# Picked tokens fetched by number, and a changed order in the heads, the convolution and the end of the merge, in a two-layer diffusion step

## What is computed

```python
g = jax.nn.sigmoid(gt.reshape(bsz, n_tok, N_BRANCH, D_MODEL))
merged = g[:, :, 0] * (y_ml @ w_pa) + g[:, :, 1] * (y_cv @ w_pb) + g[:, :, 2] * (y_na @ w_pc)
return merged @ w_o, (c_s, n_s, m_s), nk, nv

def expert_choice_ffn(h, w_router, w_gate, w_up, w_down):
    cap = EC_CAPACITY_FACTOR * n_tok // N_EXPERTS
    aff = jax.nn.softmax((h @ w_router).astype(jnp.float32), axis=-1)
    gate, idx = lax.top_k(jnp.swapaxes(aff, 1, 2), cap)
    xg = jax.vmap(lambda hb, ib: hb[ib])(h, idx)
    a = jnp.einsum('becd,edf->becf', xg, w_gate)
    u = jnp.einsum('becd,edf->becf', xg, w_up)
    y = jnp.einsum('becf,efd->becd', jax.nn.silu(a) * u, w_down) * gate[..., None].astype(h.dtype)
    return jax.vmap(lambda yb, ib: jnp.zeros((n_tok, d), h.dtype).at[ib.reshape(-1)].add(
        yb.reshape(-1, d)))(y, idx)
```

## Time and profile before

| | us |
|---|---|
| median of 3 runs | 3190.81 |
| lowest, highest | 3184.38, 3193.99 |
| the profiled execution | 3193.39 |
| its span, first to last instruction | 3191.6 |
| mean granted clock of PE | 0.951 |
| PE busy, DVE busy, ACT busy, POOL busy in the span | 2995.6, 1876.5, 1357.6, 546.3 |

### The profile page before, as it was taken

How to read it: one execution, slowest core, us unless ns; L and a number is a source line. 1 busy time by engine, 2 the same in 40 slices (tenths; PEclk the granted TensorE clock), 3 DMA queues, 4 the chain that set the end, 5 groups by cost and what they waited for, 6 DMA issues and landing times.

```text
span 3191.6 us, 42921 instructions
## 1 busy us (share of the span) xinstructions
PE 2995.6 (94%) x17920; PEld 2461.0 (77%) x17920; DVE 1876.5 (59%) x2079; ACT 1357.6 (43%) x1751; POOL 546.3 (17%) x218
## 2 busy tenths in 40 slices
PE   4999989999997999999989998899999799999998
PEld 2979877999896676767659798899999766676765
DVE  4542644324316989888865427341351488989897
ACT  2133230111106767777741432310110577777775
POOL 2413213233211000000024133152332100000000
PEclk7989899999988999999989898799998799999999
DMA  8523447557514989898985234332443198989896
GB/s 232 73 34 60 87 113 198 131 161 172 136 70 147 345 285 343 279 346 282 344 225 75 32 64 83 73 67 40 80 80 113 55 348 296 327 296 329 300 324 235
DMA packets 357650, 580.80 MB, mean 182 GB/s; under 512 B 13712, under 2 KB 148880, under 8 KB 357328
## 3 DMA queue, kind: packets, MB, share of 16 engines
q1 hardware_dynamic: 297488, 501.26, 53.8%
q10 hardware_dynamic: 51808, 56.53, 5.6%
q0 software_dynamic: 8160, 20.26, 2.0%
HBM read 568.54 MB, written 9.45 MB: 181 GB/s over the span
## 4 chain that ended last, share of the span: by engine, by line
PE 76%; DVE 8%; DMA 7%; issue 3%; ACT 2%; DVEq 2%; SPq 1%; ACTq 0%; POOL 0%; POOLq 0%
PE ps L826 27%; PE ps L1310 8%; PE ps L1313 8%; PE ps L1318 8%; PE ps L792 5%; DMA ring<-w_down 3%; PE ps L1227 2%; DVE w_lo L2242 2%; PE ps L868 2%; PE ps L1088 2%; DVEq L1969 2%; DMA ring<-w_gate 1%; PE ps L900 1%; ACT w_hi L1440 1%; PE ps L1005 1%
## 5 line engine op out<-in xcount | busy, mean ns | idle before, releaser
L2242 DVE TENSOR_TENSOR w_lo<-ring,w_hi 128x2048 fp32r<-128x2048 f32 x256 | 584.3, 2287 | 99.3 <-ACT w_hi L1440 98.6
L826 PE MATMUL ps<-h_hi,w_hi 128*128 128x320 f32 x1792 | 560.2, 313 | 3.7 <-DVE arena L2020 2.0
L826 PE MATMUL ps<-h_lo,w_hi 128*128 128x320 f32 x1792 | 555.6, 310 | 0.0
L826 PE MATMUL ps<-h_hi,w_lo 128*128 128x320 f32 x1792 | 555.6, 310 | 0.0
L1440 ACT ACTIVATE w_hi<-ring 128x2048 fp32r<-128x2048 f32 x256 | 486.6, 1909 | 82.7 <-DMA ring<-w_up 24.5
L671 POOL CAST w_hi<-ring 128x2048 fp32r<-128x2048 f32 (+1 forms) x76 | 143.0, 1881 | 1607.0 <-DMA ring<-w_in 1007.6
L1500 ACT ACTIVATE arena<-ps,par 128x640 f32<-128x640 f32 x88 | 70.0, 796 | 705.3 <-PE ps L826 675.7
L673 POOL TENSOR_TENSOR w_lo<-ring,w_hi 128x2048 fp32r<-128x2048 f32 (+1 forms) x76 | 345.7, 4548 | 29.3 <-issue 28.5
L826 PEld LDWEIGHTS ps<-h_hi,w_hi 128*128 128x128 f32 x1792 | 338.4, 189 | 6.3 <-issue 3.9
L826 PEld LDWEIGHTS ps<-h_lo,w_hi 128*128 128x128 f32 x1792 | 338.2, 189 | 0.5 <-issue 0.5
L826 PEld LDWEIGHTS ps<-h_hi,w_lo 128*128 128x128 f32 x1792 | 338.0, 189 | 0.0
(11 more groups left out here) (311 smaller groups left out, 5472.5 us busy)
## 6 DMA issues: line engine op xcount, KB each, us to landing
ring<-w_gate SPq DMA_DIRECT2D x128, 1024.0 KB, 5.8
ring<-w_up SPq DMA_DIRECT2D x128, 1024.0 KB, 6.2
ring<-w_down SPq DMA_DIRECT2D x128, 1024.0 KB, 6.9
ring<-w_in SPq DMA_DIRECT2D x64, 1024.0 KB, 13.1
arena<-ada_w ACTq DMA_DIRECT2D x40, 1024.0 KB, 6.2
arena<-ada_w SPq DMA_DIRECT2D x8, 1024.0 KB, 15.5
arena<-biasT ACTq DMA_DIRECT2D x16, 512.0 KB, 6.0
ring<-w_o SPq DMA_DIRECT2D x8, 1024.0 KB, 14.6
```

What stands on the lines that cost most here:

```text
L826: last = pe.matmul(ps[:, bank(u) + half, 0:HALF], w[:, k, f0:f0 + P], a[:, k, at], start=(k == 0 and part == 0), stop=(k == KD - 1 and par ...
L2242: dve.tensor_tensor(w_los[g % NW], ring[:, s, :], w_his[g % NW].bitcast(F32), ALU.subtract).then_inc(slot_used[s], 1)
```

## The change

Six places change.

1. In `ada_first` the turn of chunk 3 comes right behind the sums of squares, not behind the rows of chunk 4; POOL splits the second chunk of the first projection only behind the last `h_split`.
2. In layer 1 the four stores of x have a semaphore each, and `norm_high` waits for the pair that it writes over.
3. In the convolution the ada turns of a boundary stand behind the next unit, not in front of it; so does the turn in front of the first gate. DVE's `mod_add`s move with `ada_adds`, and those of the tenth convolution unit go into the merge's first turn. The last ada turn of the merge stands in front of the last branch unit.
4. W_O's first half-unit waits for the columns of `merged` one by one, and its banks are shifted by one pair.
5. ACT writes the tokens as `h_tok` alone, POOL stores them to `tok_copy` in memory (five transfers). `gate_cols` now has two columns, the gate and the token's number, and runs before the fetch: in front of the first one, and behind chunk 2 of the last expert of a quad (`picks` moves from chunk 3 to chunk 1). DVE copies the numbers out (`picked_cols`), POOL fetches 80 rows of 4 KB for each of the four experts with indirect transfers, and `gather` is four transposes for each block dt.
6. Some semaphores go (`cond_zeroed`, `rcol_ready`, `cc_ready`).

```diff
                 if l == 0:
-                    split(l, R_MQ)
+                    split(l, R_MQ, 1)
+                    pool.wait_ge(*h_split.at(l, KD))
+                    split(l, R_MQ + 1, 1)
...
                 for t in range(NTILE):
                     pool.wait_ge(*tok_copied.at(l, 2 * t + 2))
-                    pool.tensor_tensor(tok_lo[:, t, :], h_tok[:, t, :], tok_hi[:, t, :].bitcast(F32),
-                                       ALU.subtract).then_inc(tok_low.sem, 1)
+                    pool.dma_start(tok_dram[t * P:(t + 1) * P, :], h_tok[:, t, :]).then_inc(tok_stored.sem, 16)
+                pool.wait_ge(*tok_stored.at(l, NTILE))
+                for quad in range(NQUAD):
+                    pool.wait_ge(*gate_col_ready.at(l, quad + 1))
+                    if quad:
+                        pool.wait_ge(*gather_ps.at(l, KD * quad))
+                    pool.sem_inc(pool_passed, 1)
+                    for i in range(4):
+                        pool.indirect_dma_start(xg_tok[0:CAP, i, :], None, tok_dram[:, :],
+                                                bass.IndirectOffsetOnAxis(tok_idx[0:CAP, i:i + 1], 0))\
+                            .then_inc(tok_landed.sem, 16)
...
                     for k in range(KD):
+                        if fresh and half == 0:
+                            pe.wait_ge(*merged_ready.at(l, 2 * KD + k + 1))
...
-                    if n:
+                    if n and n != 4:
                         ada_turn(n - 1)
                     if n == 3:
...
+                        ada_turn(3)
...
             def convolution(l):
                 for v in range(3 * KB):
-                    if v and l == 0:
-                        for n in ada_conv(v - 1):
-                            ada_turn(n)
                     if v % 2 == 0:
                         _, hi, lo = split_chunk(l, R_CONV + v // 2)
                     split_unit(l, U_CV[v], hi, lo, v % 2 * P)
                     if l == 0:
+                        for n in ada_conv(v - 1) if v else ():
+                            ada_turn(n)
                         for n in ada_conv(v):
                             ada_later(n)
...
-                out = ps[:, GATHER_BANK[dt], 0:4 * CAP].rearrange("p (e c) -> p e c", e=4)
-                at = slice(dt * P, (dt + 1) * P)
-                for t in range(1, NTILE):
-                    for part, tok in enumerate((tok_hi, tok_lo)):
-                        pe.matmul(out[:, :, 0:CAP_S], tok[:, t, at], pick_s[:, t - 1, :, :],
-                                  start=(t == 1 and part == 0), stop=(t == NTILE - 1 and part == 1))
-                for part, tok in enumerate((tok_hi, tok_lo)):
-                    last = pe.matmul(out[:, :, CAP_S:CAP], tok[:, 0, at], pick_p[:, :, 0:CAP_P],
-                                     start=(part == 0), stop=(part == 1))
+                for i in range(4):
+                    last = pe.transpose(ps[:, GATHER_BANK[dt], i * CAP:(i + 1) * CAP],
+                                        xg_tok[0:CAP, i, dt * P:(dt + 1) * P], ident[0:CAP, 0:CAP])
                 last.then_inc(gather_ps.sem, 1)
...
-                    if i == 0 and c == 0:
-                        gate_cols(l, quad)
+                    if i == 3 and e < NE - 1 and c == 2:
+                        gate_cols(l, quad + 1)
...
-                        ada_adds(6 * j + 2 + f, 6 * j + 1 + f if f else max(6 * j - 1, 0))
+                        ada_adds(6 * j + 1 if f else max(6 * j - 2, 0), 6 * j + 1 + f)
...
-                        ada_adds(6 * j + 4 + f, 6 * j + 3 + f)
+                        ada_adds(6 * j + 2 + f, 6 * j + 3 + f)
...
-                        for n in (ada_of(i - 1),) if i else ada_conv(3 * KB - 1):
+                        for n in (ada_of(i - 1),) if i else (*ada_conv(3 * KB - 2), *ada_conv(3 * KB - 1)):
                             mod_add(n)
```

More of the change, by code:

```diff
@@ L204, in step_program @@
             pass
-        tok_hi = sb("tok_hi", [P, NTILE, D], F32R)
-        tok_lo = sb("tok_lo", [P, NTILE, D], F32R)
+        h_tok = sb("h_tok", [P, NTILE, D])
+        xg_tok = sb("xg_tok", [P, 4, D])
+        tok_idx = sb("tok_idx", [P, 4], mybir.dt.uint32)
         xg_hi = sb("xg_hi", [P, KD, 4, CAP], F32R)
@@ L315, in step_program @@
         y_p = ff(128, D)
[L316 to L320, removed]
+        aff_tok = ff(1152, NTILE, NE + 1)
+        aff = aff_tok[:, :, 0:NE]
+        posT = ff(1240, NTILE, NE)
+        smax = ff(1320, NTILE)
+        gate_col = ff(1328, 2, 4)
         zeros = view(FF_AT - 3200, T)
@@ L356, in step_program @@
         x_summed = signal("x_summed", 1)
-        x_saved = signal("x_saved", 4, 16)
+        x_saved = [signal(f"x_saved{i}", 1, 16) for i in range(KD // 2)]
         x_back = signal("x_back", 1, 16)
@@ L514, in bank @@
         def bank(u):
-            return 2 * ((u - U_WO) % 3) if U_WO <= u < U_WO + KD else 2 * (u % 4)
+            return 2 * ((u - U_WO + 2) % 3) if U_WO <= u < U_WO + KD else 2 * (u % 4)
         def filled(l, u):
@@ L748, in _ @@
                 if l:
-                    pool.wait_ge(*x_saved.at(l - 1, 4))
+                    for i in range(KD // 2):
+                        pool.wait_ge(*x_saved[i].at(l - 1, 1))
                 pool.sem_inc(pool_passed, 1)
@@ L814, in split_chunk, with split_unit @@
                                          for w in (w_hi, w_lo))
-            def split_unit(l, u, hi, lo, f0, acts=(h_hi, h_lo)):
+            def split_unit(l, u, hi, lo, f0, acts=(h_hi, h_lo), fresh=False):
                 if not U_WO <= u < U_WO + KD:
@@ L1132, in merge @@
                 for i in range(3 * KD):
-                    if l == 0:
-                        for n in (ada_of(i - 1),) if i else ada_conv(3 * KB - 1):
-                            ada_turn(n)
+                    if l == 0 and i:
+                        ada_turn(ada_of(i - 1))
                     if i % 2 == 0:
@@ L1139, in merge @@
                     if l == 0:
+                        for n in ada_conv(3 * KB - 1) if i == 0 else ():
+                            ada_turn(n)
                         ada_later(ada_of(i))
+                        if i == 3 * KD - 1:
+                            ada_turn(ada_of(i))
                     branch_unit(l, i // KD, i)
-                if l == 0:
-                    ada_turn(len(ADA_ALL) - 1)
             def mix_out(l):
@@ L1170, in products @@
                                   start=False, stop=False)
-                pe.wait_ge(*merged_ready.at(l, 24))
                 if l == 0:
                     pe.wait_ge(mod_ready, len(ADA_ALL))
+                pe.wait_ge(*emptied(l, U_GATE[3 * KD - 1]))
                 for j in range(4):
@@ L1391, in _ @@
                 pe.wait_ge(*posT_ready.at(l, 1))
-                pe.wait_ge(*tok_low.at(l, NTILE))
+                gate_cols(l, 0)
                 for dt in range(KD):
@@ L1489, in norm_high @@
                     act.wait_ge(mod_ready, ADA_FIRST // 2 + k // 2 + 1)
-                elif k == 0:
-                    act.wait_ge(*scale_ready.at(l, 1))
-                    act.wait_ge(*x_saved.at(l - 1, 4))
+                else:
+                    if k == 0:
+                        act.wait_ge(*scale_ready.at(l, 1))
+                    act.wait_ge(*x_saved[k // 2].at(l - 1, 1))
                 for g, (lo, hi) in enumerate(SEG):
@@ L1763, in _ @@
                     at = slice(half * 512, (half + 1) * 512)
-                    act.activation(tok_hi[:, t, at], ps[:, n % 4, :], ACT.Copy, scale=rcol[:, t:t + 1])
                     act.activation(h_tok[:, t, at], ps[:, n % 4, :], ACT.Copy, scale=rcol[:, t:t + 1])
@@ L2058, in convolution, with ada_adds @@
                 dve.memset(u_pad[:, T + 3:T + 4], 0.0)
-                def ada_adds(v, before):
-                    for slot in range(before, v) if l == 0 else ():
+                def ada_adds(first, end):
+                    for slot in range(first, end) if l == 0 else ():
                         for n in ada_conv(slot):
@@ L2106, in merge @@
                     if l == 0:
-                        for n in (ada_of(i - 1),) if i else ada_conv(3 * KB - 1):
+                        for n in (ada_of(i - 1),) if i else (*ada_conv(3 * KB - 2), *ada_conv(3 * KB - 1)):
                             mod_add(n)
+                        if i == 3 * KD - 1:
+                            mod_add(ada_of(i))
                     dve.wait_ge(*emptied(l, U_GATE[i]))
@@ L2127, in merge @@
                 if l == 0:
-                    mod_add(len(ADA_ALL) - 1)
                     dve.drain()
@@ L2259, in expert @@
                         add_context(l, quad - 1)
-                    if i == 3 and e < NE - 1 and c == 3:
+                    if i == 3 and e < NE - 1 and c == 1:
                         picks(l, quad + 1)
```

61 lines of the change are left out of this document (37 added, 24 removed).

## The result

The changed kernel takes 3243.57 us (median of 4 runs) against 3188.51 for the kernel before on the same chip: a ratio of 1.0171, 95% interval 1.0144 to 1.0198. It is slower by 1.7%, where 1% faster was forecast. The profiled execution grew from a span of 3191.6 to one of 3246.1, by 54.5 us, and its two traces tell where. The table has the shift of the same instruction of PE between the two, from stage to stage; the rows add up to the 54.5. Differences of that size say little by themselves.

A forecast was written before the change was run, and what follows sets the result against it. PE was taken as the bound (76% of the chain), with DMA close behind in the experts. Terms -9.7 - 3.9 + 5 + 10 - 9.5 + 6 - 30 = -32.1 gave 3158 us against the median; range 3128 to 3196.

The forecast's parts named there:

- Experts: Three later fetches in each layer: transposes replace PE's gather products, -5 us each, -30 in all.
- The price of the transposes: Expert fetches: 32 pipelined transposes at .07 us apiece, 2.2 in all, where products cost PE 9.25.
- The DMA term: Experts: DMA has room, 552 of 600 us plus 12 for three fetches; 2 us taken off per fetch.
- The rival on the DMA: Experts: DMA becomes the bound, 5 us off per fetch instead of 2; -12 for -30, 3177 us; chance 0.12.
- the margin: Experts, layer 0: 15 us in 600 between DMA's and PE's new times, so only single chunks come late.
- The rival of the late landing: Fetches: POOL's issues wait out DVE's `w_lo`, tokens land late, PE waits; +5.6 us a fetch, 3239; chance 0.12.
- Routes: Route and first fetch in each layer: the new chain from `gate_cols` to `gathered_hi` costs +3 us.
- Convolution and merge start: Layer 0: PE waits for later `mod_add`s, +5 us in the convolution and +10 before the first gate.
- Heads: Layer starts: PE's first projection begins earlier, -9.7 us in layer 0 and -3.9 in layer 1.
- ends of the merge: W_O's first half-unit waits for single `merged` columns: -4.0 us in layer 0, -5.5 in layer 1.

The follow-up runs named there:

- half-products kernel: The kernel before, with the gather's products for the lo part of the tokens left out (5 of 10 per block): 3195.19 us, 1.0016.
- three kernels whose route is unchanged: The kernel before with heads and merge ends alone (3162.08 us), convolution order alone (3215.86), or that order with one unit's adds moved (3203.05).
- the kernel with the adds moved: The kernel before with the changed convolution order, but the tenth unit's two `mod_add`s ahead of `merge_lows`: 3203.05 us, 1.0034.
- the convolution alone: The kernel before with only the changed order of the convolution and of the merge's first turn: 3215.86 us, 1.0074.
- the fetch alone: The kernel before with only the fetch by number (tokens to memory, indirect transfers, transposes, `gate_cols` ahead): 3242.28 us, 1.0146.
- rows of 1 KB: The changed kernel with the fetches of quads 1 to 3 cut from rows of 4 KB to 1 KB: 3211.46 us, 1.0068.

## Why the prediction was wrong

**Experts: the step that failed.** Forecast -30, measured +27.4. The step took PE's products for the price of a gather and gave nearly all of it back. The half-products kernel shows that the price stood twice, on PE and on ACT. The prediction had the earlier trace rows, where PE is busy all the time, and concluded that PE alone sets it. PE busy 99% only says that PE would be late first; it does not say how far behind the next one is. The prediction itself gave the eight `gathered_hi` 11 us in the route, between ACT's start and the second chunk, and nothing here, without a reason. In the trace of before they take 19.6 us at expert 3, 1.3 us each among three `w_hi` of 1.9 and the outputs, and `gate_cols` of the kernel before needed the seventh no more than 0.3 us after it was ready. The gain was bounded by that. The price of the transposes was right: 0.55 us for eight at the first chunk.

**The DMA term** was a share over 600 us: 0.92 of them, and 12 us more. The rival on the DMA put 3 us more on a fetch. Each fetch took more, some 6 by the estimate above, at one place, where four chunks stand in a row; the four loads went from 7.0 to 11.4 us, and PE waited 15.6 us in layer 0 for the `act_row` behind them (six waits). The step that was mis-sized is the margin: an average over a stage can't pay for a burst.

**The rival of the late landing** gave nearly the right time (3239) by luck. It said that PE waits for the tokens; it never did in the quads 1 to 3. The rows it rested on came out mild: an issue took 0.89 us. Eleven of the 32 started while a `w_lo` or `w_third` of DVE ran; they took 2.05 to 2.66 and ended 0.76 to 0.86 after that operation. It was the first issue of every fetch and three others. The Trainium skill's rule (SBUF — State Buffer, the box on the "DVE blocks DMA" trap in "SBUF: two separate sides") holds in that, and its price here is 1.9 us a fetch in the mean, not 4 x 2.29.

**Routes: right sign, wrong size,** +8.4 and +10.5 for +3. (The three kernels whose route is unchanged are 4.6 or 4.7 shorter than the trace of before in the row of layer 0, so +8.4 may be +13.) The last landing came 12.9 us after `gate_cols` (1003.22 to 1016.07), where I had taken 5 to 9.5: four issues took 5.8 and not 2.75, and the landing 6.8 where I had leaned to the lower half of 2.3 to 6.7. `gate_cols` took 4.4 and not 2.9: the granted clock was 0.50 from 998.80 to 1003.30, with PE nearly idle in the 20 us before, while the 2.9 had been read at the higher clock, behind the products.

**Convolution and merge start: right mechanism, +23.8 for +15.** The waits are those that were named: before units 3 and 9 some 3.5, the gate 11.0. What was mis-sized is the price after a wait. From its first matmul to its last the units behind the waits ran for 8.83, 9.89 and 9.42 us, at a granted clock of 0.81, 0.71 and 0.75, where 7.3 is usual, as with the 8.80 in the earlier trace rows; that adds 1.5 to 2.6 each, 6.3 of the 8.8 that are missing. The prediction knew this row and used it for W_O and as a remark on the gate. The price isn't certain: in the kernel with the adds moved, unit 3 ran for 7.31 at a clock of 1.00 behind the same wait.

**Heads, ends of the merge: right** within 0.5 and 1.4 us. The 4.7 that got lost in the attention are not of the change: the kernels with the convolution alone and the fetch alone, whose heads are unchanged, lose 4.8 and 4.5 in the same stretch, and the one with rows of 1 KB, which up to there is the changed kernel, gains 4.2. The granted clock of PE goes with it: from 400 to 456 it is 0.94 in the trace of before, 0.77 in the changed kernel's and 1.00 in that with rows of 1 KB.

## What to carry to other kernels

Before pricing work that is taken from the engine that is always busy, take the length of the next engine's chain in the same stretch, and how long before its use the result is ready; the gain ends there, and a kernel that halves the work without any other change measures it in one run. Where a ring of loads runs at nine tenths, price a new transfer by the loads that are under way when it comes, not by the stage's average. When work is moved behind something on one engine, list what waits on the counter it feeds: two tiny `mod_add`s behind a long group cost 13 us here.

## What the runs showed of the hardware

Rows of 4 KB, fetched with indirect transfers to 80 partitions, bring the sum of all transfers from some 400 to some 250 GB/s while they run. Such a transfer costs POOL 0.89 us to issue, 2.05 to 2.66 when it begins under a `w_lo` or `w_third` of DVE, and it lands 6.7 to 11.5 us later; in the kernel with rows of 1 KB, which keeps 4 KB in the first fetch of a layer, 5.9 to 8.8.
